# Unnormalised queries and keys, block-diagonal matrices and a second output buffer in a gated delta-rule scan

## The reference, cut to what matters

```python
def l2_normalize(x):
    return x * lax.rsqrt(jnp.sum(x * x, axis=-1, keepdims=True) + EPS)

# gdn_branch: q, k, v = silu(conv(...)) in heads
q = l2_normalize(q.reshape(shp)) * (GDN_HD ** -0.5)
k = l2_normalize(k.reshape(shp))
...
# gdn_direction, per chunk of 64
kb = kc * bc[..., None]
lower = jnp.where(strict, jnp.einsum("nbhid,nbhjd->nbhij", kb, kc) * decay, 0.0)
rhs = jnp.concatenate([vc * bc[..., None], kb * jnp.exp(gc)[..., None]], axis=-1)
sol = lax.linalg.triangular_solve(lower + eye, rhs, left_side=True, lower=True)
...
def step(state, inp):
    v_new = ui - jnp.einsum("bhcd,bhde->bhce", wi, state)
    scores = jnp.einsum("bhqd,bhkd->bhqk", qi, ki) * di
    out = (jnp.einsum("bhcd,bhde->bhce", qi * jnp.exp(gi)[..., None], state)
           + jnp.einsum("bhqk,bhke->bhqe", scores, v_new))
    ...
# gdn_branch
o = o_f + o_b
o = o * lax.rsqrt(jnp.mean(o * o, axis=-1, keepdims=True) + EPS) * norm_g
```

## Time and profile before

| | |
|---|---|
| time, median of 3 runs | 1720.21 us (1720.06 to 1721.04) |
| the profiled execution | 1722.33 us, span 1720.5 us |
| PE busy | 1686.4 us, 98% |
| DVE busy | 1159.8 us, 67% |
| ACT busy | 950.6 us, 55% |
| layer 0, gated delta branch and scan | about 28 to 174 us of the span |
| layer 1, the same | about 358 to 501 us |

### The profile page before, as it was taken

How to read it: one execution, slowest core, us unless ns; L and a number is a source line. 1 busy time by engine, 2 the same in 40 slices (tenths; PEclk the granted TensorE clock), 3 DMA queues, 4 the chain that set the end, 5 groups by cost and what they waited for, 6 DMA issues and landing times.

```text
span 1720.5 us, 24757 instructions
## 1 busy us (share of the span) xinstructions
PE 1686.4 (98%) x10226; PEld 1389.9 (81%) x10226; DVE 1159.8 (67%) x1833; ACT 950.6 (55%) x1475; POOL 10.1 (1%) x22
## 2 busy tenths in 40 slices
PE   8999999999999999999999999999999999999998
PEld 7777888877778887888888888888888888878886
DVE  6976885679688667555686467655575556885554
ACT  7734644477155446444566667544464456974443
POOL 0000000000000000000000000000000000000000
PEclk9999999999999999999999999999999999999999
DMA  6322445543234555555544325555555555445543
GB/s 261 123 76 99 166 151 197 184 169 102 85 141 150 192 182 188 188 191 179 218 178 152 115 107 186 222 191 186 211 192 187 196 198 206 147 169 186 193 175 146
DMA packets 41872, 291.70 MB, mean 170 GB/s; under 512 B 4672, under 2 KB 4928, under 8 KB 7712
## 3 DMA queue, kind: packets, MB, share of 16 engines
q1 hardware_dynamic: 39312, 280.68, 45.3%
q0 software_dynamic: 2304, 8.91, 1.5%
q10 hardware_dynamic: 144, 0.52, 0.1%
HBM read 289.05 MB, written 1.05 MB: 169 GB/s over the span
## 4 chain that ended last, share of the span: by engine, by line
PE 81%; DVE 13%; ACT 3%; issue 2%; DMA 1%; SPq 0%; DVEq 0%; ACTq 0%
PE pg L476 24%; PE pg L478 24%; PE pg L477 24%; DVE wl L1946 3%; PE ps L824 2%; PE ps L643 2%; ACT wh L1316 1%; DMA raw<-weights 1%; PE ps L867 1%; PE ps L627 0%; DVE hTl L2517 0%; PE ps L926 0%; PE ps L1211 0%; PE ps L1166 0%; PE ps L1096 0%
## 5 line engine op out<-in xcount | busy, mean ns | idle before, releaser
L476 PE MATMUL pg<-wh,hTh 128*128 128x512 f32 x2096 | 835.3, 399 | 3.9 <-DVE wl L1979 1.9
L478 PE MATMUL pg<-wh,hTl 128*128 128x512 f32 x2096 | 818.4, 390 | 0.0
L477 PE MATMUL pg<-wl,hTh 128*128 128x512 f32 x2096 | 817.6, 390 | 0.0
L1946 DVE TENSOR_TENSOR wl<-raw,wh 128x1024 fp32r<-128x1024 f32 x518 | 609.4, 1220 | 190.3 <-ACT wh L1316 187.2
L1316 ACT ACTIVATE wh<-raw 128x1024 fp32r<-128x1024 f32 x528 | 528.7, 1054 | 201.1 <-DMA raw<-weights 190.8
L476 PEld LDWEIGHTS pg<-wh,hTh 128*128 128x128 f32 x2096 | 394.1, 188 | 88.6 <-issue 8.4
L478 PEld LDWEIGHTS pg<-wh,hTl 128*128 128x128 f32 x2096 | 393.9, 188 | 84.2
L477 PEld LDWEIGHTS pg<-wl,hTh 128*128 128x128 f32 x2096 | 394.5, 188 | 75.3
L1411 ACT ACTIVATE arena<-pg,sm 128x256 f32<-128x256 f32 (+1 forms) x67 | 36.6, 546 | 241.7 <-PE pg L478 241.6
L2604 DVE SCALAR_TENSOR_TENSOR arena<-pg,sm,arena 128x256 f32<-128x256 f32 x88 | 38.5, 479 | 157.7 <-ACT arena L1412 157.7
L1371 ACT ACTIVATE hTh<-ps 128x512 fp32r<-128x512 f32 x60 | 33.6, 597 | 31.0 <-PE ps L643 31.0
(11 more groups left out here) (384 smaller groups left out, 1143.1 us busy)
## 6 DMA issues: line engine op xcount, KB each, us to landing
raw<-weights SPq DMA_DIRECT2D x265, 1024.0 KB, 4.8
arena<-wide POOLq DMA_DIRECT2D x9, 512.0 KB, 3.6
raw<-weights SPq DMA_DIRECT2D x2, 512.0 KB, 5.7
cst<-const_tables POOLq DMA_DIRECT2D x1, 1024.0 KB, 5.2
plainh<-dist_tables POOLq DMA_DIRECT2D x2, 512.0 KB, 5.6
arena<-gate_mix POOLq DMA_DIRECT2D x1, 1024.0 KB, 6.1
x<-x_in ACTq DMA_DIRECT2D x1, 512.0 KB, 3.9
x<-x_in SPq DMA_DIRECT2D x1, 512.0 KB, 8.9
```

Source lines behind the costliest of these rows:

```text
L476: pe.matmul(dst, lh, rh, start=first, stop=False)
L477: pe.matmul(dst, lh, rl, start=False, stop=False)
L478: return pe.matmul(dst, ll, rh, start=False, stop=last)
L1946: tt(wl[:, slot, h], raw[:, slot, h], wh[:, slot, h], ALU.subtract)\
```

## The change

- Queries and keys are no longer normalised. The outputs of silu for q and k are in `qnT` and `knT` from the start, so the normalising products and `features` go. ACT copies the raw keys, turned back, to `kn`. The norms are made once for both (`norms`, behind the third convolution on DVE) and enter elsewhere: values are multiplied by beta and the key's norm (on DVE L2158's successor, on ACT four small operations in each of four levels), the lower triangle's mask and the state term (`NEGS`) by beta and its square, and the result by the query's norm.
- The inverse and the scores are written into block-diagonal matrices, 128x128 per head, with one direction in each half (`diagonal(t)`). GpSimd sets the other blocks to zero, 16 memsets a layer, after the layer's `rs_ready`. The multiplication by beta behind the inverse goes. A set of PE is 4 products of the whole array in place of 8 on 64x64 tiles. ACT copies a quarter of the inverse (`inv_copied`).
- The output of the last two visits goes to a buffer of its own (`X_`); one addition behind the scan (`o_sum`) joins the two.
- The retention masks are made in parts: three multiplies at the old place, the fourth and the fused ones in the levels and behind the first visit; their exponential goes from ahead of the levels to ACT's second visit (t = 1).
- `SC_`, `LMASK`, `squares` lie elsewhere; a weight split ahead of the scan (two `prepare` calls of DVE) goes behind `VN` of the first visit.

```diff
+        T_DIAG = (TB, spare(plainl, 8))
...
+        def diagonal(t):
+            cols = 512 * (t % 2)
+            return (heads(v) for v in (T_DIAG[t // 2][:, cols:cols + 512], SC_DIAG[:, 512 * t:512 * t + 512]))
...
# PE
-                prepare(3)
-                c.wait("qk_ready")
-                features(kn, 2)
-                prepare(3)
-                c.wait("feat_read")
+                prepare(6)
+                c.wait("sq_ready")
+                c.wait("kn_ready")
                 turn_back(2)
...
+                        rhs = RV[:, h * P:(h + 1) * P] if t else VS[:, 0, h * P:(h + 1) * P]
+                        last = pe.matmul(ps[:, 0, h * P:(h + 1) * P], t_diag[:, h, :], rhs, start=True, stop=True)
...
# ACT
-                c.wait("mask_arg")
-                act.activation(MASKS, MASKS, ACT.Exp).then_inc(sem["mask_ready"], 1)
...
+                    if level < 4:
+                        for h in range(NH):
+                            v, o = VS[half(r), t, h * P:(h + 1) * P], 8 * m + 4 * d + h
+                            last = act.activation(v, v, ACT.Copy, scale=BETA_NK[half(r), o:o + 1])
...
+                    if t == 1:
+                        c.wait("mask_arg")
+                        act.activation(MASKS, MASKS, ACT.Exp).then_inc(sem["mask_ready"], 1)
...
# DVE
+                def norms():
+                    c.wait("sq_ready", 2)
+                    c.step(dve.tensor_reduce(NORMS, squares.rearrange("p (k e) -> p k e", e=HD), AX.X, ALU.add))
+                    rstd_of(NORMS, 1.0)
+                    c.step(ts(NQ, NQ, HD ** -0.5, None, ALU.mult))
+                    tt(NQ2, NQ, NQ, ALU.mult)
+                    ...
...
-                normalized(0, qn)
...
-                normalized(1, kn)
                 gemm(D, (512,), ("evac_act",), ahead=2)
                 later_taps(2)
+                norms()
                 prepare(7)
...
-                retention_masks(l)
+                for h in range(3):
+                    last = retention_mask(h)
+                c.step(last)
...
+                for r in range(2):
+                    tt(SC6[half(r), :, r, :, half(r)], SC5[half(r), 0], QK4[half(r)], ALU.mult)
+                    for m in range(M):
+                        last = tt(SC6[half(r), 1 - m, 1 - r, :, half(r)], SC5[half(r), 1, m], QK4[half(r), m], ALU.mult)
...
+                        c.step(both_ways(i - 1) if i else retention_mask(3))
...
-                prepare(1)
-                prepare(1)
...
-                    for _ in range(2 if t else 1):
+                    if t == 0:
+                        both_ways(3).then_inc(sem["mask_arg"], 1)
+                    for _ in range(2 if t else 3):
                         prepare(1)
...
-                    if t >= 2:
-                        for d in range(2):
-                            m, r = scan_chunk(t, d)
-                            last = tt(OT[half(r), :], OT[half(r), :], O3[half(r), m, :], ALU.add)
...
# GpSimd
+                pool.wait_ge(sem["rs_ready"], l + 1)
+                for t in range(4):
+                    for v in diagonal(t):
+                        for r in range(2):
+                            last = pool.memset(v[half(r), :, half(1 - r)], 0.0)
+                last.then_inc(sem["zeros_ready"], 1)
```

More of the change, by code:

```diff
@@ L891, in gdn @@
                     for h in range(NH):
-                        for d, m, r in places[t]:
-                            last = pe.matmul(ps[half(r), 1, h * P:(h + 1) * P], SC4[half(r), 4 * d + h, m, :],
-                                             VN[half(r), h * P:(h + 1) * P], start=True, stop=True)
+                        last = pe.matmul(ps[:, 1, h * P:(h + 1) * P], sc_diag[:, h, :], VN[:, h * P:(h + 1) * P],
+                                         start=True, stop=True)
                     last.then_inc(sem["sv_done"], 1)
@@ L1473, in gdn @@
                 prepare(5)
-                features(knT, 2)
                 convolved(2)
@@ L2193, in pair_mask @@
                     return MASK[name].unsqueeze(1).unsqueeze(1).broadcast_to([P, 2, 4, CHUNK])
+                c.wait("cum_exp")
+                for t in range(1, 4):
+                    for d in range(2):
+                        m, r = scan_chunk(t, d)
+                        o = 8 * m + 4 * d
+                        last = stt(NEGS[half(r), 4 * t:4 * t + 4], EGS[half(r), 4 * t:4 * t + 4], -1.0,
+                                   BETA_NK2[half(r), o:o + 4], ALU.mult, ALU.mult)
+                c.step(last)
                 c.wait("low_t")
@@ L2233, in gdn @@
-                for g in range(2):
-                    q = slice(8 + 4 * g, 12 + 4 * g)
-                    last = tt(TB3[:, q, :], X5[:, g, 1], over(BETAJ[:, q], CHUNK), ALU.mult)
-                c.sig(last, "inv_scaled")
-                prepare(1)
-                prepare(1)
-                c.wait("cum_exp")
-                c.step(ts(NEGS, EGS, -1.0, None, ALU.mult))
-                O3 = o_acc.rearrange("p (m e) -> p m e", m=M)
+                        old, new = (v.rearrange("p g (h m f) -> p m g h f", m=M, f=CHUNK)
+                                    for v in (X_.rearrange("p (g n) -> p g n", g=2)[:, :, 256:512], ps[:, 2:4, 256:512]))
@@ new lines, in second_direction @@
+                        def second_direction(t):
+                            m, r = scan_chunk(t, 1)
+                            dst, _ = diagonal(t)
+                            return tt(dst[half(r), :, half(r)].rearrange("p (g h) f -> p g h f", g=2), old[half(r), m],
+                                      new[half(r), m], ALU.add)
+                        second_direction(0)
+                        c.wait("inv_yt")
+                        first_old, first_new = (v.rearrange("p (h m f) -> p m h f", m=M, f=CHUNK)
+                                                for v in (XT_[:, 0:256], ps[:, 0, 0:256]))
@@ new lines, in gdn @@
+                        for t in range(4):
+                            m, r = scan_chunk(t, 0)
+                            dst, _ = diagonal(t)
+                            last = tt(dst[half(r), 0:2, half(r)], first_old[half(r), m], first_new[half(r), m], ALU.add)
+                        c.sig(last, "inv_scaled")
+                        for t in range(1, 4):
+                            last = second_direction(t)
+                        last.then_inc(sem["inv_scaled"], 1)
+                visits = [v.rearrange("p (m e) -> p m e", m=M) for v in (o_acc, X_)]
```

125 lines of the change are left out of this document (60 added, 65 removed).

## The result

The changed kernel takes 1725.53 us in the median of 22 runs, the kernel before 1722.63 in 22 runs next to them; the ratio is 1.0020, with a 95% interval of 1.0013 to 1.0026. One of the changed kernel's 22 runs took 4326.60 us, more than twice the time of all others, and is left out of the ratio. So it is slower by 3.4 us (2.2 to 4.5), just at the bound of 0.2% from which a difference counts. The forecast was 1725.5, from a median of 1720.21 for the kernel before. By its own difference it was 5.3 slower; measured are 3.4. The absolute value came out exact by luck, because the kernel before, too, took 2.4 us more in these runs than in the first three.

What follows compares the result with a forecast made beforehand. The recurrence was taken to run at the pace of DVE's list, though PE is 98% busy. Two layers' 4.3 us plus 1.0 for the clock took 1722.3 to 1727.6 profiled, 1725.5 in the median; range 1714 to 1731.

Steps and rivals of the forecast that it cites:

- PE's work removed: Four sets of feature transposes save 4.7 us, 16 block-diagonal scan sets 3.7: 8.4 less for PE, if nothing else waits.
- DVE's list up to the inverse: From the third convolution on: first level of the inverse 1.6 us later a layer, bounds 0.5 and 2.5, PE waiting.
- The levels: Mask operations moved into the inverse's levels, one each, add 0.75 us a layer on the path, bounds 0 and 1.1.
- End of the inverse and scan: PE waits 2.2 and 0.4 us at the third visit, yet 0.2 ahead a layer is kept by the end.
- The table load: Ahead of the masks' exponential in ACT's second visit: 1.28 us; by the skill's 2.66 the time were 1728.3.
- The layer's sum: First level, levels and scan together: 1.6 + 0.75 - 0.2 = 2.15 us more a layer, 4.3 in two.
- Clock and idle time inside the inverse: PE's slower clock behind new waits: 1.0 us, bounds -1.9 and 5; idle gap without releaser: 0, bounds -2.9 and 3.
- A: DVE's list up to the inverse no longer than before, so PE's saving counts: 1710.7 us, with half 1715.5; 22%.
- B: Both cancel: first level only 0.5 us later, nothing lost in the levels; 1720.8 us, no change; 23%.
- D: Slow clock behind each exposed wait, 1.9 us each in three of four places: 1730.2 us; 15%.

Runs made afterwards that it cites:

- tiles_64: The changed kernel with the scan's two products a visit back on 64x64 tiles, 16 passes a set; 1725.11 us, ratio 1.0021 to the kernel before.
- negs_in_levels: The changed kernel with DVE's six small operations for the negated decay moved from ahead of the inverse to its second level; 1723.43 us, ratio 1.0008.
- norms_before_taps: The changed kernel with the norms on DVE ahead of the third convolution's later taps instead of behind them; 1722.29 us, ratio 1.0007.
- exp_behind_split: The changed kernel with the masks' exponential on ACT moved behind the second visit's weight split and reads; 1716.08 us, ratio 0.9968.

## Why the prediction was right, step by step

**PE's work removed.** The sign and the size of the saving were right, with one term low. Two sets of feature transposes took 1.16 and 1.11 us out of the traces' distance in layer 0 (forecast 1.18). A scan set saves 0.30 to 0.36, forecast 0.23 (0.21 by the rows that it names): its 8 passes took 0.81 and not 0.91, as I had priced them by the pace of 16 passes in a row. The rule of the Trainium skill on tiles (TensorEngine Tiling (Array Packing), Tiling Modes) was weighed rightly: the 64-row form of tiles_64 takes 1.02 us for 16 passes, so they run in pairs, and half the passes do not halve the set.

**DVE's list up to the inverse.** Right in nearly each term. The taps of the third convolution began at 59.19 (forecast 59.2), the norms ended at 68.6 (68.6), PE got the weights behind 2.96 us of waiting at 70.0 (3.3, at 69.8), the diagonal scores and their gaps took 2.76 (2.8), the negated decay 0.82 (0.7). The first level came 1.45 us later in layer 0 and 1.56 in layer 1; forecast 1.6. That this list sets it, and not PE or ACT, the wait for L2224 says, and negs_in_levels and norms_before_taps bear it out: the first level came sooner in both.

**The levels.** Forecast 0.75 a layer, measured 0.3 and 0.4 by the weight products outside the idle times. DVE's masked product of the fourth level came 0.7 later against the first (118.50 - 96.35 against 115.98 - 94.52), but PE's planned products cover part of it.

**End of the inverse and scan.** From the levels to the first state product 1.3 us sooner in layer 1 (forecast 1.2). The wait at the third visit 2.45 and 0.26 to 0.33 (forecast 2.2 and 0.4), by the mechanism given: table load and exponential ahead of ACT's split. exp_behind_split shows it. From the end of the levels to the transposes of the result the change is 0.4 ahead in layer 1 (forecast 0.2).

**The table load.** The exponential starts at 144.26, behind a load at 142.96 of 1.28, with no drain between. By the figure of the Trainium skill (ScalarE: Activation LUTs, What ACT_TABLE_LOAD costs), 2.66, PE's wait would have been 1.4 us longer than the 2.45 here; the trace does not agree with the figure.

**The layer's sum.** Layer 1, which has one idle time inside the inverse in both kernels, grows by 1.64 us (forecast 2.15): levels 0.3 less, scan 0.2 less. Layer 0 gets 0.7 shorter.

**Clock and idle time inside the inverse.** These are the terms that were off: "0, bounds -2.9 and 3" for the idle time and "1.0" for the clock. The idle time of layer 0 (1.60) is gone. In the profiled pair the clock came out about even in what it cost: of two slow stretches that have gone, the one behind that idle time (122 us) had cost some 1.5 us; three have come, each behind a new wait as I had put it (at 70, at 397 and at 151 us), and of these the one at 151 cost 1.2. The two behind the wait for the weights are hidden, as forecast: in exp_behind_split that stretch lies some 5 us later, the wait ahead of the first level is 1.6 in place of 2.6, and the level starts within 0.3 us of the same time. So of the 1.4 us by which the spans differ 0.38 are there at the first weight product, before the change touches anything; layer 0 gives back 0.71, layer 1 adds 1.64, and the rest of the program nearly nothing.

In the medians the change costs 2 us more than in this pair, and the clocks of the runs can account for it: the profiled execution has a mean of 0.995, the median of the runs 0.993, and at 1.2 us for 0.001 that is an estimate of 2.4 us; measured are 1.85. The kernel before has 0.997 in the median of its later runs; for the 22 beside the changed kernel no clock is on record. So the sum came near for a reason that is half luck. The path was forecast at 4.3 and is 3.3 (twice the 1.64), the idle time at 0 and is -1.6 in this pair, and the clock at 1.0 and is some 2 in the medians. Why the clock is lower in most runs of the changed kernel is only argued, by the waits that it falls behind; the same wait at the third visit is followed by 0.57 in layer 0 and by 1.00 in layer 1 of one execution.

**The rivals.** A (faster) would have needed 1.6 us less in DVE's list; it was within 0.2 of my sum. B needed a first level 0.5 us later and nothing lost in the levels; the levels lost 0.3 to 0.4, but the first level was 1.5 late. D's slow stretches were there behind three of the waits, but the one whose price was measured cost 1.2 us (exp_behind_split), not 1.9, two were hidden, and two of the kernel before had gone. One price that I had not seen is that of the second output buffer: I gave it next to nothing, and without it the change would cost 0.28% more. And of the block-diagonal form I counted 3.7 us, of which tiles_64 finds nothing left in the changed kernel.

Open stays what the unnormalised queries and keys bring alone, which wasn't tried.

## What to carry to other kernels

A work item that moves off one critical list has to be followed to the place where it lands: the masks' exponential of 3.2 us was put ahead of a weight split with no slack, while 4.8 us of idle time on the same engine stood just behind that split. Where PE's work is cut ahead of a wait for another engine, the wait grows by what was cut; so look for the wait first, remove it, and only then is the shorter product worth its time (0.4 us less against 4.6 more for the longer product here, each with 2 us or more to each side). And where a wait is new, compare the granted clock of many runs and not only that of two traces. And a wait that one removes by reordering one engine's list alone comes back further down the queue, unless work goes into that engine's own idle time.

## What the runs showed of the hardware

- Four float32 products of 128x128 by 128 columns, 8 passes, take 0.81 us from the first to the next product; eight on 64x64 tiles, 16 passes, 1.02. The entry behind a weight product is 0.23 and 0.32 us.
- Behind a wait of 2.4 to 3.0 us PE's clock goes to 1.2 GHz in some places and not in others: in the changed kernel in layer 0 at the third visit (0.57 of full clock in 151 to 155 us), not in layer 1 at the same one (1.00 in 480 to 484). Where PE sets the pace it costs 0.9 to 1.5 us for one such stretch (norms_before_taps at 421 and 479 us, exp_behind_split against the changed kernel at 151, the kernel before at 122), and nothing where PE waits for DVE behind it.
- Among executions of one kernel the time follows the mean granted clock: 1.2 us for 0.001 in the changed kernel, from 0.991 to 0.995, and about 1.0 in the kernel before, from 0.993 to 0.999.
- Inside a set of 128 passes of 64x64 products PE stood still for 0.4 to 1.8 us behind the same pass, 108, in kernels with the same number of passes, and 24 small products at the program's start moved it from one layer to the other.
- Sixteen memsets of 64x256 on GpSimd a layer, 0.31 us each and one every 0.34, ran beside DVE's weight splits, which stayed at 2.36 us for a pair.
